# Output projection of a mixer that starts with the heads' blocks ahead of the gated products, with the turns of heads and groups between its pieces

## The chip, the cores and the metric

The kernel runs on one core of a Trainium2 chip. The metric is the device time of one execution in microseconds (us). TensorE (PE in the profile; PEld are its weight loads), VectorE (DVE), ScalarE (ACT) and GpSimd (POOL) each work through their own instructions in order and wait for one another on semaphores; SyncE (SP) issues the loads of the weight stream.

## What is computed

The kernel is two transformer blocks on a sequence of 1024 rows of width 1024, all in float32. The change lies in the mixer of the second block:

```python
proj = h @ w_mix_in[l]
q, k, v, u = jnp.split(proj, [ATTN_WIDTH, 2 * ATTN_WIDTH, 3 * ATTN_WIDTH], axis=-1)
attn = dilated_attention(q, k, v).astype(x.dtype)            # 8 heads of 64: 512 columns
...
# s5_mixer(u): 32 groups of 16 channels: 512 columns
y = jax.nn.gelu(y.reshape(B, S, SSM_WIDTH))
return y * jax.nn.sigmoid(y @ w_glu.astype(f32) + b_glu.astype(f32))
...
mixed = jnp.concatenate([attn, ssm], axis=-1) @ w_mix_out[l]
x = x + rms_norm_2(mixed, mix_post_g[l])
```

The output projection `mixed` sums over 1024 channels. The first 512 come from the attention heads, the last 512 from the gated groups.

## The kernel before

**Products.** Every large product is made in three matmuls (lines 126, 127, 128, in `products`): each operand is kept as a high part and the rest (`hi` and `lo`), and hi·hi, hi·lo and lo·hi are summed in PSUM. ACT makes the high part with a copy, DVE then makes the rest with a subtraction (for a weight unit that is `make_hi`, L117, and `make_lo`, L121). PSUM has eight banks of 128x512.

**Weight stream.** All large weights come in units of 128x1024 (512 KB), in one fixed order, through two staging buffers `raw`. SP issues the load of unit n when unit n-2 is ready, that is when its `make_lo` has ended (semaphore `unit_ready`). For this mixer the stream has two units for the gate (`glu_unit(0)`, `glu_unit(1)`, written to `glu_w`) and then eight for the output projection (called `mixo`, slots `A[:, 0]` to `A[:, 7]` of `region_a`). Two blocks of 128 channels share a unit, and the second four units are the other 512 output columns.

**Attention** (`att_pe`, `att_act`, `att_dve`). A loop over 64 pairs (head, row tile) has scores, the maximum, the exponential, transposes of the probabilities (L1642), and the sum of values (`values`, L1652), whose result DVE scales into `O` (`att_o`, L1719; semaphore `at_o`). Between them stand the steps of the state-space groups (L1422 to L1431), whose last result ACT writes to `U` (L1463, semaphore `s5_g`).

**Turns.** `O` and `U` have rows on the partitions; the products need channels there. So PE turns each of them in eight pieces: a piece q is four 128x128 transposes into one PSUM bank, for block j = q // 2 and half of the rows q % 2. For the heads (L1673), ACT copies the piece to `B` (`region_b`, L1707), DVE writes its rest (L1740). The PE turns piece q when piece q-2 has been read (`ot_lo`), as there are two banks. For the groups (L1499), ACT applies GELU (L1520, semaphore `yt_f`) and after every second piece makes the high part (L1524); DVE makes the rest (L1539, `yt_lo`) in `YH`, the second half of `region_a`.

**Gate and projection.** `glu_pe` waits for all of that and has 8 groups of 12 matmuls (32x3 in all). After each, ACT applies the sigmoid (L1530, `gl_s`), DVE multiplies (L1547), ACT and DVE split the result into blocks 4 to 7 of `B` (L1533, L1549, `gl_lo`). Then `wide_pe` makes the projection: for each of the 8 channel blocks i, six row tiles of the first output half, 18 matmuls a block and 144 in all, in PSUM banks 0 to 5; then the ten other (row tile, half) pairs with 24 matmuls each. ACT and DVE reach `wide_hi(act, mixo, range(8))` and `wide_lo(dve, mixo, range(8))` after all of the gate's work.

Of the kernel before, what the change touches and what calls it, by code (L numbers as in the profile page):

```python
# [5 lines left out]
P = 128  # L6
S = 1024
D = 1024
NT = S // P
KD = D // P  # L10
HALF = 512
# [33 lines left out]
def program(nc, x, p, stream, cols, rows, gate_mats, pool_mats, inv_count, ssm_g, ssm_bc, x_mid, ssm_mid, att_mid, out):  # L45
    f32 = mybir.dt.float32
# [6 lines left out]
    with ctx:  # L53
# [1433 lines left out]
        def eighths(X, half):  # L1487

            return X.rearrange("p (c t) -> p t c", t=GT)[:, 4 * half:4 * half + 4, :]

        def glu_pe(pe):
            pe.wait_ge(s5_g, 8)
            for q in range(8):
                j, half = divmod(q, 2)
                if q >= 2:
                    pe.wait_ge(yt_f, q - 1)
                for t in range(4):
                    tt_ = 4 * half + t
                    last = nc.tensor.transpose(ps[:, 2 + q % 2, t * P:(t + 1) * P],  # L1499
                                               U[:, tt_, j * P:(j + 1) * P], ident[:, :])  # L1500
                last.then_inc(yt_tr, 1)
            pe.wait_ge(ot_lo, 8)
            pe.wait_ge(yt_lo, 8)
            pe.wait_ge(unit_ready, U_GLU + 2)
            for g in range(8):
                j, half = divmod(g, 2)
                if g >= 4:
                    pe.wait_ge(gl_s, g - 3)
                slot = glu_w[:, j // 2]
                for k in range(4):  # L1510
                    c0 = (j % 2) * HALF + k * P
                    last = products(ps[:, (0, 1, 4, 5)[g % 4], :], lambda h: slot[:, h, c0:c0 + P],
                                    lambda h: YH[:, k, h, half * HALF:(half + 1) * HALF], k == 0, k == 3)
                last.then_inc(gl_done, 1)

        def glu_act(act):
            for q in range(8):
                j, half = divmod(q, 2)
                act.wait_ge(yt_tr, q + 1)
                nc.scalar.activation(eighths(yf[:, j, :], half), ps[:, 2 + q % 2, :].rearrange("p (t c) -> p t c", t=4),  # L1520
                                     ACT.Gelu_apprx_tanh).then_inc(yt_f, 1)
                if half:
                    act.wait_ge(yt_f, q + 1)
                    nc.scalar.activation(YH[:, j, 0, :], yf[:, j, :], ACT.Copy).then_inc(yt_hi, 1)  # L1524
            for g in range(8):
                j, half = divmod(g, 2)
                act.wait_ge(gl_done, g + 1)
                if g >= 2:
                    act.wait_ge(gl_p, g - 1)
                nc.scalar.activation(sg[:, g % 2, :], ps[:, (0, 1, 4, 5)[g % 4], :], ACT.Sigmoid,  # L1530
                                     bias=c_("b_glu", j)).then_inc(gl_s, 1)
# [4 lines left out]
        def glu_dve(dve):  # L1536
            for j in range(4):
                dve.wait_ge(yt_hi, j + 1)
                nc.vector.tensor_tensor(YH[:, j, 1, :], yf[:, j, :], YH[:, j, 0, :].bitcast(f32),  # L1539
                                        ALU.subtract).then_inc(yt_lo, 2)  # L1540
            for g in range(8):
                j, half = divmod(g, 2)
                cut = slice(half * HALF, (half + 1) * HALF)
                dve.wait_ge(gl_s, g + 1)
                if g >= 2:
                    dve.wait_ge(gl_lo, g - 1)
                nc.vector.tensor_tensor(pr_[:, g % 2, :], yf[:, j, cut], sg[:, g % 2, :], ALU.mult).then_inc(gl_p, 1)  # L1547
                dve.wait_ge(gl_hi, g + 1)
                nc.vector.tensor_tensor(B[:, 4 + j, 1, cut], pr_[:, g % 2, :], B[:, 4 + j, 0, cut].bitcast(f32),  # L1549
                                        ALU.subtract).then_inc(gl_lo, 1)  # L1550

# [83 lines left out]
        def att_pe(pe):  # L1635
# [31 lines left out]
            pe.wait_ge(at_o, NA)  # L1667
            for q in range(8):
                j, half = divmod(q, 2)
                if q >= 2:  # L1670
                    pe.wait_ge(ot_lo, q - 1)
                for t in range(4):
                    last = nc.tensor.transpose(ps[:, q % 2, t * P:(t + 1) * P],  # L1673
                                               O[:, 4 * half + t, j * P:(j + 1) * P], ident[:, :])
                last.then_inc(ot_tr, 1)

        def att_act(act):
            def rest(n):
# [10 lines left out]
            for n in range(NA):  # L1689
# [6 lines left out]
                if n:  # L1696
                    rest(n - 1)
                    ssm_step_act(act, n - 1)
            link_act(act, nc.scalar.activation(small[:, 1:2], eps, ACT.Gelu_apprx_tanh))
            rest(NA - 1)  # L1700
            ssm_step_act(act, NA - 1)
            for u in range(2):
                hi_of(act, glu_unit(u))
            for q in range(8):
                j, half = divmod(q, 2)
                act.wait_ge(ot_tr, q + 1)
                nc.scalar.activation(B[:, j, 0, half * HALF:(half + 1) * HALF], ps[:, q % 2, :],  # L1707
                                     ACT.Copy).then_inc(ot_hi, 1)

        def att_dve(dve):  # L1710
            link = lambda ins: link_dve(dve, ins)
# [11 lines left out]
            for n in range(NA):  # L1723
# [10 lines left out]
            for u in range(2):  # L1734
                lo_of(dve, glu_unit(u))
            for q in range(8):
                j, half = divmod(q, 2)
                dst = B[:, j, :, half * HALF:(half + 1) * HALF]
                dve.wait_ge(ot_hi, q + 1)
                nc.vector.tensor_tensor(dst[:, 1, :], ps[:, q % 2, :], dst[:, 0, :].bitcast(f32),  # L1740
                                        ALU.subtract).then_inc(ot_lo, 1)


        mix_out = sem("mix_out")
# [255 lines left out]
        def _(act):  # L2000
# [47 lines left out]
        def _(dve):  # L2048
# [20 lines left out]
            proj_dve(dve)  # L2069
            att_dve(dve)  # L2070
            glu_dve(dve)
            wide_lo(dve, mixo, range(8))
# [7 lines left out]
        def _(pe):  # L2080
# [12 lines left out]
            glu_pe(pe)  # L2093
            wide_pe(pe, mixo, lambda i: pe.wait_ge(gl_lo, max(2, 2 * i - 6)), n_ffn2)
            feed_pe(pe, ffn2, n_ffn2, ({}, {}))


# [102 lines left out]
```

## Time and profile before

| | |
|---|---|
| time, median of 3 runs | 3254.61 us (3253.44 to 3259.25) |
| time of the profiled execution | 3254.53 us |
| its span | 3252.7 us (1.8 us of the time lies outside it) |
| mean granted TensorE clock | 0.976 |
| PE busy | 3089.1 us, 95% |
| DVE, ACT busy | 1380.0 us (42%), 868.3 us (27%) |
| last pair of the attention to the first product of the projection | 2345.16 to 2400.07 us |

The span is the time from the first to the last recorded instruction; all times below are us from its start. A granted clock of 1.0 is TensorE at full speed, 0.5 half of it. A busy PE is not a PE at its peak, since the ends of overlapping matmuls are modelled; the distance between two starts says more than the duration.

### The profile page before, as it was taken

To read this page: it belongs to the slowest core of one execution; us is meant where nothing else is said; L and a number is where in the kernel's file an instruction comes from. 1 tells how busy PE (TensorE), PEld (TensorE's weight loads), DVE (VectorE), ACT (ScalarE), POOL (GpSimd) and SP (SyncE) were. 2 spreads that over 40 slices of the span, in tenths; PEclk is the share of its full clock that TensorE was granted. 3 is DMA by queue.
4 is the path that set the end of the run, shared out by engine and by line. 5 is a ranking of instruction groups with operands and counts; after the bars stand their busy time and mean duration, and the time that the engine had idled before them with its cause. 6 is when DMAs were issued, how large, how long until landed. Compare 5 with 4: busy or idle time off the path is not lost.

```text
span 3252.7 us, 36883 instructions
## 1 busy us (share of the span) xinstructions
PE 3089.1 (95%) x14144; PEld 2546.1 (78%) x14144; DVE 1380.0 (42%) x1783; ACT 868.3 (27%) x1316; POOL 408.2 (13%) x1012
## 2 busy tenths in 40 slices
PE   7999999999998989999999989988888999999997
PEld 5777888888887777888888878877767888888885
DVE  5654444444445443333333363244435233333335
ACT  5523222211123342111121241144434211121112
POOL 0000000000000004888800000011101000000001
PEclk9999999999999999999999999989989999999998
DMA  3121111111111121232211221111113111111113
GB/s 121 39 78 65 59 52 52 45 39 45 52 52 39 52 72 48 90 109 83 88 45 64 97 85 65 70 66 48 38 65 117 59 46 40 51 58 45 39 52 117
DMA packets 54410, 206.99 MB, mean 64 GB/s; under 512 B 7216, under 2 KB 7984, under 8 KB 52000
## 3 DMA queue, kind: packets, MB, share of 16 engines
q1 hardware_dynamic: 37440, 136.33, 12.1%
q0 software_dynamic: 16864, 69.22, 5.8%
q8 instruction: 70, 1.15, 0.1%
q14 instruction: 36, 0.29, 0.0%
HBM read 173.15 MB, written 31.20 MB: 63 GB/s over the span
## 4 chain that ended last, share of the span: by engine, by line
PE 90%; DVE 5%; ACT 2%; issue 2%; DMA 0%; SPq 0%; POOL 0%; DVEq 0%; ACTq 0%
PE ps L126 28%; PE ps L128 27%; PE ps L127 27%; PE ps L1652 2%; PE ps L262 1%; PE ps L1616 1%; PE ps L1642 1%; DVE acc L815 1%; DVE region_b L121 1%; PE ps L1422 1%; DVE acc L177 1%; DVE acc L185 1%; PE ps L1417 0%; ACT region_b L117 0%; PE ps L1429 0%
## 5 line engine op out<-in xcount | busy, mean ns | idle before, releaser
L126 PE MATMUL ps<-region_a,region_b 128*128 128x512 f32 x1664 | 659.3, 396 | 19.4 <-DVE region_a L221 9.8
L127 PE MATMUL ps<-region_a,region_b 128*128 128x512 f32 x1664 | 651.7, 392 | 0.0
L128 PE MATMUL ps<-region_a,region_b 128*128 128x512 f32 x1664 | 651.4, 391 | 0.0
L815 DVE TENSOR_TENSOR acc<-acc,ps 128x1024 f32<-128x1024 f32 x288 | 351.1, 1220 | 332.6 <-PE ps L128 332.6
L126 PE MATMUL ps<-region_b,region_a 128*128 128x512 f32 x1088 | 433.3, 398 | 17.3 <-DVE region_b L121 9.9
L127 PE MATMUL ps<-region_b,region_a 128*128 128x512 f32 x1088 | 428.7, 394 | 0.0
L128 PE MATMUL ps<-region_b,region_a 128*128 128x512 f32 x1088 | 428.7, 394 | 0.0
L121 DVE TENSOR_TENSOR region_b<-raw,region_b 128x1024 fp32r<-128x1024 f32 x176 | 216.1, 1243 | 394.8 <-ACT region_b L117 394.4
L126 PEld LDWEIGHTS ps<-region_a,region_b 128*128 128x128 f32 x1664 | 314.9, 189 | 87.6 <-issue 10.0
L128 PEld LDWEIGHTS ps<-region_a,region_b 128*128 128x128 f32 x1664 | 314.7, 189 | 65.9
L127 PEld LDWEIGHTS ps<-region_a,region_b 128*128 128x128 f32 x1664 | 315.0, 189 | 64.8 <-issue 1.7
L126 PE MATMUL ps<-region_b 128*128 128x512 f32 x896 | 353.3, 394 | 8.6 <-DVE acc L811 4.8
L127 PE MATMUL ps<-region_b 128*128 128x512 f32 x896 | 350.7, 391 | 0.0
L128 PE MATMUL ps<-region_b 128*128 128x512 f32 x896 | 350.7, 391 | 0.0
L126 PEld LDWEIGHTS ps<-region_b,region_a 128*128 128x128 f32 x1088 | 215.7, 198 | 61.0 <-issue 10.1
L128 PEld LDWEIGHTS ps<-region_b,region_a 128*128 128x128 f32 x1088 | 215.4, 198 | 40.9
L127 PEld LDWEIGHTS ps<-region_b,region_a 128*128 128x128 f32 x1088 | 215.9, 198 | 39.2
L117 ACT ACTIVATE region_b<-raw 128x1024 fp32r<-128x1024 f32 x176 | 181.5, 1050 | 160.0 <-DMA raw<-stream 130.1
L726 ACT ACTIVATE rtmp<-ps 128x512 f32<-128x512 f32 x88 | 52.7, 598 | 630.2 <-PE ps L128 630.1
L126 PEld LDWEIGHTS ps<-region_b 128*128 128x128 f32 x896 | 169.5, 189 | 45.3 <-DVE acc L811 5.2
L121 DVE TENSOR_TENSOR region_a<-raw,region_a 128x1024 fp32r<-128x1024 f32 x74 | 89.5, 1224 | 261.0 <-ACT region_a L117 261.0
L128 PEld LDWEIGHTS ps<-region_b 128*128 128x128 f32 x896 | 169.3, 189 | 35.4
(286 smaller groups left out, 3343.9 us busy)
## 6 DMA issues: line engine op xcount, KB each, us to landing
raw<-stream SPq DMA_DIRECT2D x252, 512.0 KB, 3.2
ssm_row<-ssm_mid POOLq DMA_DIRECT2D x8, 1632.0 KB, 7.1
x_mid<-acc POOLq DMA_DIRECT2D x24, 512.0 KB, 3.0
ssm_mid<-made_osc POOLq DMA_DIRECT2D x8, 1024.0 KB, 4.5
ssm_mid<-made_out POOLq DMA_DIRECT2D x8, 608.0 KB, 3.5
acc<-x SPq DMA_DIRECT2D x8, 512.0 KB, 7.9
rold<-x POOLq DMA_DIRECT2D x16, 256.0 KB, 3.6
old_a<-x_mid POOLq DMA_DIRECT2D x8, 512.0 KB, 8.6
```

The lines of the kernel that those rows point to most:

```text
L117: nc.scalar.activation(slot[:, 0, :], raw[:, odd, :], ACT.Copy).then_inc(hi_done, 1)
L121: nc.vector.tensor_tensor(slot[:, 1, :], raw[:, odd, :], slot[:, 0, :].bitcast(f32), ALU.subtract).then_inc(unit_ready, 1)
L126: nc.tensor.matmul(psum, lhs(0), rhs(0), start=first, stop=False)
L127: nc.tensor.matmul(psum, lhs(0), rhs(1), start=False, stop=False)
L128: return nc.tensor.matmul(psum, lhs(1), rhs(0), start=False, stop=last)
L177: nc.vector.scalar_tensor_tensor(out=acc[:, t, :], in0=acc[:, t, :], scalar=rinv_post[:, t:t + 1], in1=gb[:, N.post, :], op0=ALU.mult, op1 ...
L185: nc.vector.scalar_tensor_tensor(out=a, in0=a, scalar=N.factor, in1=N.old(t), op0=ALU.mult, op1=ALU.add).then_inc(N.sem["res"], 1)
L262: last = nc.tensor.transpose(ps[:, 6 + d % 2, t * P:(t + 1) * P], xn[:, t, d * P:(d + 1) * P], ident[:, :])
L726: nc.scalar.activation(rtmp[:, half, :], ps[:, up_bank(c, j, half), :], ACT.Silu).then_inc(F.sem["ge"], 1)
L815: nc.vector.tensor_tensor(acc[:, t, :], acc[:, t, :], src, ALU.add).then_inc(F.sem["de"], 1)
L1422: last = nc.tensor.matmul(bank[i], zt[:, s - 4, i * P:(i + 1) * P], zt[:, 2, i * P:(i + 1) * P], start=True, stop=True)
L1652: last = nc.tensor.matmul(ps[:, 6, 0:HEAD_DIM], probT[:, n % 2, k, :], V[:, k, h * HEAD_DIM:(h + 1) * HEAD_DIM], start=k == 0, stop=k == i)
```

## The change

PE no longer turns all heads, then all groups, then makes the gate's products, then all of the projection. The heads' first two pieces (block 0, of heads whose values were long done) are turned before the last `values`, into banks 4 and 5. Two more follow. Then the projection begins with blocks 0 to 3 (the heads'), cut into eight pieces of three row tiles (9 matmuls each), with two turns behind each of the first six pieces: the heads' last four and the groups' eight, all in banks 6 and 7. Then come the gate's products, now in banks 6 and 7 in place of 0, 1, 4 and 5 (so a group waits for the sigmoid of the group before the last), and then blocks 4 to 7 of the projection. What stands behind them is the same.

On ACT and DVE the high part and the rest of gate unit 0 move ahead of the attention's last step, those of `mixo` units 0 and 1 stand among the heads' turns (behind pieces 2 and 4), and those of units 2 and 3 among the gate's results (behind groups 1 and 3). Units 4 to 7 stay behind the gate. The stream's order is the same; a unit's load is still tied to the unit two ahead of it being ready. The number of matmuls, copies and loads does not change.

```diff
+        TURN_BANKS = (4, 5) + (7, 6) * 7
+
+        def turn_heads_pe(pe, q):
+
+            j, half = divmod(q, 2)
+            if q < 2:
+                pe.wait_ge(at_pt, NA)
+            elif q == 2:
+                pe.wait_ge(s5_g, NB)
+            elif q == 3:
+                pe.wait_ge(at_o, NA)
+            else:
+                pe.wait_ge(ot_lo, q - 1)
+            pe.wait_ge(at_o, 2 * NT * (j + 1))
+            for t in range(4):
+                last = nc.tensor.transpose(ps[:, TURN_BANKS[q], t * P:(t + 1) * P],
+                                           O[:, 4 * half + t, j * P:(j + 1) * P], ident[:, :])
+            last.then_inc(ot_tr, 1)
+
+        def turn_groups_pe(pe, q):
+
+            j, half = divmod(q, 2)
+            pe.wait_ge(*((yt_f, q - 1) if q >= 2 else (ot_lo, 7 + q)))
...
         def glu_pe(pe):
...
+            pe.wait_ge(yt_f, 8)
             pe.wait_ge(yt_lo, 8)
-            pe.wait_ge(unit_ready, U_GLU + 2)
             for g in range(8):
                 j, half = divmod(g, 2)
-                if g >= 4:
-                    pe.wait_ge(gl_s, g - 3)
+                if g >= 2:
+                    pe.wait_ge(gl_s, g - 1)
...
+        def mixo_pe(pe):
...
+            turns = [lambda q=q: turn_heads_pe(pe, q) for q in range(4, 8)]
+            turns += [lambda q=q: turn_groups_pe(pe, q) for q in range(8)]
+            turn_heads_pe(pe, 2)
+            turn_heads_pe(pe, 3)
+            for k in range(4):
+                pe.wait_ge(unit_ready, U_MIXO + k // 2 + 1)
+                pe.wait_ge(ot_lo, 2 * k + 2)
+                for part_of in range(2):
+                    for t in range(3 * part_of, 3 * part_of + 3):
+                        part(0, t, k, k == 0, False)
+                    for turn in turns[4 * k + 2 * part_of:4 * k + 2 * part_of + 2]:
+                        turn()
+            glu_pe(pe)
+            for k in range(4, KD):
+                pe.wait_ge(unit_ready, U_MIXO + k // 2 + 1)
+                pe.wait_ge(gl_lo, 2 * k - 6)
+                for t in range(6):
+                    ins = part(0, t, k, False, k == KD - 1)
...
         def glu_act(act):
+            for q in range(8):
+                turn_heads_act(act, q)
+                if q == 2 or q == 4:
+                    wide_hi(act, mixo, [q // 2 - 1])
...
                 nc.scalar.activation(B[:, 4 + j, 0, half * HALF:(half + 1) * HALF], pr_[:, g % 2, :],
                                      ACT.Copy).then_inc(gl_hi, 1)
+                if g == 1 or g == 3:
+                    wide_hi(act, mixo, [2 + g // 2])
...
+            turn_heads_pe(pe, 0)
+            turn_heads_pe(pe, 1)
             values(NA - 1)
...
+            lo_of(dve, glu_unit(0))
             finish(NA - 1)
-            for u in range(2):
-                lo_of(dve, glu_unit(u))
...
+            lo_of(dve, glu_unit(1))
...
-            wide_hi(act, mixo, range(8))
+            wide_hi(act, mixo, range(4, 8))
```

PE's instructions from the last `values` on, before. `att_o` are the heads' outputs, `u` the groups', `ident` the identity of a transpose; the waits of an instruction stand in brackets.

```order
L1652 MATMUL ps<-v,probT 128x64 [waits at_o,at_pt]
L1652 MATMUL ps<-v,probT 128x64 x7
L1673 MATMUL ps<-ident,att_o 128x128 [waits at_o]
L1673 MATMUL ps<-ident,att_o 128x128 x7
L1673 MATMUL ps<-ident,att_o 128x128 [waits ot_lo]
L1673 MATMUL ps<-ident,att_o 128x128 x3
```

The same place in the changed kernel:

```order
L1506 MATMUL ps<-ident,att_o 128x128 [waits at_o,at_pt]
L1506 MATMUL ps<-ident,att_o 128x128 x3
L1733 MATMUL ps<-v,probT 128x64 [waits at_o,at_pt]
L1733 MATMUL ps<-v,probT 128x64 x7
L1506 MATMUL ps<-ident,att_o 128x128 [waits at_o,s5_g]
L1506 MATMUL ps<-ident,att_o 128x128 x3
L1506 MATMUL ps<-ident,att_o 128x128 [waits at_o]
L1506 MATMUL ps<-ident,att_o 128x128 x3
L126 MATMUL ps<-region_a,region_b 128x512 [waits ot_lo,unit_ready]
L127 MATMUL ps<-region_a,region_b 128x512
L128 MATMUL ps<-region_a,region_b 128x512
```

A piece of the heads' turn now stands ahead of the last `values`, and the first matmul of the projection stands behind the fourth turn, with a wait for a weight unit.

ACT's instructions at the same place, before (`glu_w` the gate's weights, `L1699` the load of GELU's table, L1463 the last group's result):

```order
L1699 ACT_TABLE_LOAD
L1699 ACTIVATE small<-small 128x1
L1684 ACTIVATE probT<-ps 128x1024 [waits at_pv,at_tr,act_chain]
L1463 ACTIVATE u<-ps 128x4x8x16 [waits s5_y]
L117 ACTIVATE glu_w<-raw 128x1024 [waits at_s,raw_full0]
L117 ACTIVATE glu_w<-raw 128x1024 [waits at_s,raw_full1]
L1707 ACTIVATE region_b<-ps 128x512 [waits ot_tr] x8
```

And in the changed kernel:

```order
L117 ACTIVATE glu_w<-raw 128x1024 [waits at_s,raw_full0]
L1773 ACT_TABLE_LOAD
L1773 ACTIVATE small<-small 128x1
L1757 ACTIVATE probT<-ps 128x1024 [waits at_pv,at_tr,act_chain]
L1463 ACTIVATE u<-ps 128x4x8x16 [waits s5_y]
L117 ACTIVATE glu_w<-raw 128x1024 [waits at_s,raw_full1]
L1577 ACTIVATE region_b<-ps 128x512 [waits ot_tr] x3
L117 ACTIVATE region_a<-raw 128x1024 [waits at_pv,raw_full0]
L1577 ACTIVATE region_b<-ps 128x512 [waits ot_tr] x2
L117 ACTIVATE region_a<-raw 128x1024 [waits at_pv,raw_full1]
L1577 ACTIVATE region_b<-ps 128x512 [waits ot_tr] x3
```

Gate unit 0 moved ahead of the table load, and the first two units of the projection (`region_a<-raw`) moved in among the eight copies of the heads' pieces. DVE's queue is cut in the same way.

## Rows read from the trace of the kernel before

**Rows 1.** The page: span, and the chain that ended last, by engine.
```profile
span 3252.7 us, 36883 instructions
PE 90%; DVE 5%; ACT 2%; issue 2%; DMA 0%; SPq 0%; POOL 0%; DVEq 0%; ACTq 0%
```

**Rows 2.** Busy time by stretch: PE, PEld, DVE, ACT, POOL, granted clock, DMA share, GB/s.
```profile
2347.10:2357.00 9.90, 6.30 (x34) 5.08 (x34) 6.60 (x10) 4.07 (x7) 0.00 (x0) 0.75 0.32 106
...
2367.20:2371.50 4.30, 0.00 (x0) 0.03 (x1) 2.42 (x2) 4.13 (x4) 1.11 (x2) 0.50 0.64 229
2371.50:2395.60 24.10, 24.10 (x96) 19.46 (x96) 9.56 (x14) 9.26 (x14) 0.00 (x0) 0.91 0.01 4
```

**Rows 3.** PE in order of time: start, us, instruction, idle time before and its releaser.
```profile
2345.16 1.97 PE L1652 MATMUL ps<-v,probT 128*128 128x64 f32 x16 [0.54 <-DVE att_o L1719]
2347.58 1.09 PE L1673 MATMUL ps<-ident,att_o 128*128 128x128 f32 x8 [0.45 <-DVE att_o L1719]
...
2371.50 0.77 PE L126 MATMUL ps<-region_a,glu_w 128*128 128x512 f32 x1 [4.35 <-issue]
...
2376.18 0.39 PE L128 MATMUL ps<-region_a,glu_w 128*128 128x512 f32 x1
...
2395.22 0.39 PE L128 MATMUL ps<-region_a,glu_w 128*128 128x512 f32 x1
2400.07 0.77 PE L126 MATMUL ps<-region_a,region_b 128*128 128x512 f32 x1 [4.46 <-DVE region_a L121]
...
2403.48 0.39 PE L128 MATMUL ps<-region_a,region_b 128*128 128x512 f32 x1
```

**Rows 4.** ACT in order of time, the same columns.
```profile
2342.92 0.60 ACT L1463 ACTIVATE u<-ps 128x512 f32<-128x512 f32 x1 [3.16 <-PE ps L1431]
...
2348.27 1.09 ACT L1707 ACTIVATE region_b<-ps 128x512 fp32r<-128x512 f32 x2 [2.86 <-PE ps L1673]
...
2360.93 2.04 ACT L1520 ACTIVATE yf<-ps 128x512 f32<-128x512 f32 x2
2362.99 1.06 ACT L1524 ACTIVATE region_a<-yf 128x1024 fp32r<-128x1024 f32 x1
...
2370.09 1.28 ACT L1530 ACT_TABLE_LOAD   x1
2376.61 0.69 ACT L1530 ACTIVATE sg<-ps,col 128x512 f32<-128x512 f32 x1 [5.23 <-PE ps L128]
```

**Rows 5.** DVE in order of time, the same columns.
```profile
2344.73 0.28 DVE L1719 TENSOR_SCALAR att_o<-ps,stats 128x64 f32<-128x64 f32 x1 [4.44 <-PE ps L1652]
...
2347.44 2.35 DVE L121 TENSOR_TENSOR glu_w<-raw,glu_w 128x1024 fp32r<-128x1024 f32 x2
2349.70 1.28 DVE L1740 TENSOR_TENSOR region_b<-ps,region_b 128x512 fp32r<-128x512 f32 x2
...
2370.18 1.22 DVE L1539 TENSOR_TENSOR region_a<-yf,region_a 128x1024 fp32r<-128x1024 f32 x1 [1.78 <-ACT region_a L1524]
2377.33 0.69 DVE L1547 TENSOR_TENSOR pr<-yf,sg 128x512 f32<-128x512 f32 x1 [5.93 <-ACT sg L1530]
```

**Rows 6.** DVE and ACT on the projection's units, in order of time.
```profile
2398.70 2.36 DVE L121 TENSOR_TENSOR region_a<-raw,region_a 128x1024 fp32r<-128x1024 f32 x2 [0.25 <-ACT region_a L117]
2403.31 1.06 ACT L117 ACTIVATE region_a<-raw 128x1024 fp32r<-128x1024 f32 x1 [3.70 <-DMA raw<-stream]
```

**Rows 7.** PE where a norm's turns stand between products, in order of time.
```profile
2510.52 0.60 PE L262 MATMUL ps<-ident,xn 128*128 128x128 f32 x4
...
2511.66 0.60 PE L262 MATMUL ps<-ident,xn 128*128 128x128 f32 x4
```

**Rows 8.** Two stretches of 2 us within the turns, columns as in rows 2.
```profile
2356.00:2358.00 2.00, 2.00 (x11) 2.00 (x11) 1.02 (x2) 1.30 (x3) 0.00 (x0) 0.50 0.00 0
2360.00:2362.00 2.00, 0.64 (x4) 0.40 (x4) 0.88 (x1) 2.00 (x3) 0.00 (x0) 1.00 0.00 0
```

**Rows 9.** ACT on the last unit of the projection, in order of time.
```profile
2416.86 1.06 ACT L117 ACTIVATE region_a<-raw 128x1024 fp32r<-128x1024 f32 x1 [1.03 <-DMA raw<-stream]
```

More of the change, by code:

```diff
@@ L1489, in eighths @@
             return X.rearrange("p (c t) -> p t c", t=GT)[:, 4 * half:4 * half + 4, :]
[L1491 to L1502 removed]
+        TURN_BANKS = (4, 5) + (7, 6) * 7
[17 more added lines that the diff above has]
+            pe.wait_ge(*((yt_f, q - 1) if q >= 2 else (ot_lo, 7 + q)))
+            for t in range(4):
+                tt_ = 4 * half + t
+                last = nc.tensor.transpose(ps[:, TURN_BANKS[8 + q], t * P:(t + 1) * P],
+                                           U[:, tt_, j * P:(j + 1) * P], ident[:, :])
+            last.then_inc(yt_tr, 1)
+        def glu_pe(pe):
+            pe.wait_ge(yt_f, 8)
             pe.wait_ge(yt_lo, 8)
[L1504 removed]
             for g in range(8):
                 j, half = divmod(g, 2)
[L1507 to L1508 removed]
+                if g >= 2:
+                    pe.wait_ge(gl_s, g - 1)
                 slot = glu_w[:, j // 2]
@@ L1511, in glu_pe, with part @@
                     c0 = (j % 2) * HALF + k * P
-                    last = products(ps[:, (0, 1, 4, 5)[g % 4], :], lambda h: slot[:, h, c0:c0 + P],
+                    last = products(ps[:, 6 + g % 2, :], lambda h: slot[:, h, c0:c0 + P],
                                     lambda h: YH[:, k, h, half * HALF:(half + 1) * HALF], k == 0, k == 3)
                 last.then_inc(gl_done, 1)
+        def mixo_pe(pe):
+            def part(half, t, k, first, last):
+                slot = mixo.slots[4 * half + k // 2]
+                return products(ps[:, (NT * half + t) % 6, :],
+                                lambda h: B[:, k, h, t * P:(t + 1) * P],
+                                lambda h: slot[:, h, (k % 2) * HALF:(k % 2 + 1) * HALF], first, last)
+            turns = [lambda q=q: turn_heads_pe(pe, q) for q in range(4, 8)]
[16 more added lines that the diff above has]
+                    ins = part(0, t, k, False, k == KD - 1)
+                    if k == KD - 1:
+                        ins.then_inc(mixo.done, 1)
+            for g in range(6, 2 * NT):
+                half, t = divmod(g, NT)
+                if t == 0:
+                    pe.wait_ge(unit_ready, U_MIXO + 8)
+                pe.wait_ge(mix_out, g - 5)
+                for k in range(KD):
+                    last = part(half, t, k, k == 0, k == KD - 1)
+                    if g == NT + 6 and k % 2:
+                        norm_pe_step(pe, n_ffn2, 0, k // 2)
+                    if g == NT + 7 and k % 2 == 0:
+                        norm_pe_step(pe, n_ffn2, 0, 4 + k // 2)
+                last.then_inc(mixo.done, 1)
@@ L1534, in glu_act @@
                                      ACT.Copy).then_inc(gl_hi, 1)
+                if g == 1 or g == 3:
+                    wide_hi(act, mixo, [2 + g // 2])
         def glu_dve(dve):
+            for q in range(8):
+                j, half = divmod(q, 2)
+                dst = B[:, j, :, half * HALF:(half + 1) * HALF]
+                dve.wait_ge(ot_hi, q + 1)
+                nc.vector.tensor_tensor(dst[:, 1, :], ps[:, TURN_BANKS[q], :], dst[:, 0, :].bitcast(f32),
+                                        ALU.subtract).then_inc(ot_lo, 1)
+                if q == 2 or q == 4:
+                    wide_lo(dve, mixo, [q // 2 - 1])
             for j in range(4):
@@ L1701, in att_act @@
             ssm_step_act(act, NA - 1)
-            for u in range(2):
[L1703 to L1708, printed above, removed]
+            hi_of(act, glu_unit(1))
         def att_dve(dve):
@@ L2071, in _ @@
             glu_dve(dve)
-            wide_lo(dve, mixo, range(8))
+            wide_lo(dve, mixo, range(4, 8))
             dve_mixo(dve, ffn2_norm_hooks(dve))
```

32 lines of the change are left out of this document (12 added, 20 removed).

## Prediction

> **What bounds the kernel now.** I read the page first. The chain that ended last is PE for 90% of the span [rows 1], so time is won only where PE stands still, runs at half clock, or is given less to do. The change gives it the same matmuls. Next I read busy time by stretch around the place of the change [rows 2]: from 2347.10 to 2357.00 PE is busy 6.30 of 9.90 us, from 2367.20 to 2371.50 not at all, and the granted clock is 0.75 and 0.50 there (1.0 is 2.4 GHz, 0.50 is 1.2 GHz; 0.75 is a mean over both). Then PE in order of time [rows 3]: the heads' turns begin at 2347.58, the gate's products at 2371.50 after 4.35 us of nothing, the projection at 2400.07 after 4.46 us of nothing. In this stretch PE is paced by others: ACT has a chain of two GELUs and a high part for each block (2.04 us and 1.06 us, one directly behind the other [rows 4]), DVE ends it [rows 5], and the wait at 2400.07 is for the first unit of the projection, whose high part and rest ACT and DVE make only after the gate [rows 6].
>
> What the work itself takes: the gate's 12th matmul starts at 2376.18, its 96th at 2395.22 [rows 3], 84 steps of **0.2267 us**. The first 11 steps took 4.68 us instead of 2.49 us, so restarting at half clock cost 2.19 us. In the projection the ninth matmul starts 3.41 us after the first, where eight steps are 1.81 us: 1.60 us lost. A turn between products costs 0.455 us of PE: between two turns of a norm, 1.14 us apart [rows 7], stand three matmuls (0.68 us). From 2347.58 the old order needs, at these prices, 16 turns (7.3 us), 96 matmuls (21.8 us) and the 144 of the first six tiles (32.6 us), 61.7 us. It ends at 2403.48 + 136 x 0.2267 = **2434.3**, which is 86.7 us. So 25 us stand open to be won, and the question is how much the new order leaves.
>
> **The change, step by step.** I replay the three queues with those durations.
>
> *Start.* The values of pair 62 end just before 2344.73, when DVE scales them [rows 5]. PE now turns heads' pieces 0 and 1 (2344.45 to 2345.36, 0.9 us), then the last values (16 steps, 1.8 us, the 1.97 us row without its end [rows 3]) to 2347.16, piece 2 at once, and piece 3 after DVE's last scaling, at 2347.7 to 2348.2. The two early pieces delay the last values by 0.5 us only, since PE waited there anyway. ACT has written `U` at 2343.5 [rows 4], so piece 2 does not wait for it. The high part of gate unit 0 and the table load now lie in ACT ahead of the last `probT`, about 1 us later than before, but PE's state-space step and values of pair 62 cover it. On DVE the rest of gate unit 0 fills 2345.0 to 2346.2, where DVE had nothing to do.
>
> *The first unit.* That rest lets SP load `mixo` unit 0. The price of a load is in [rows 6]: two rests of units take 2.35 us from 2398.70, so the first is ready at 2399.93, and ACT starts on the unit that this let in at 2403.31: 3.38 us. Here: 2346.2 + 3.4 gives 2349.65; high part to 2350.7 (1.03 us); DVE, which meanwhile has the rest of gate unit 1 (2347.6 to 2348.8) and pieces 0 to 2 (0.64 us each, to 2350.8), makes the unit's rest to 2352.0. PE stands still from 2348.2 to 2352.05: **3.9 us**, a new wait for a weight unit. Behind it stands everything on PE. I expect half clock afterwards, as after 4.46 us at 2400.07, at the same 1.6 us.
>
> *Pieces with turns.* Piece one (9 matmuls, 2.04 + 1.6 us) ends at 2355.7, turns 4 and 5 at 2356.6, the next piece at 2358.65, turn 6 at 2359.1. Turn 7 needs bank 6, thus DVE's rest of head piece 5. In front of it ACT and DVE have `mixo` unit 1, behind piece 4: ACT 2356.33 to 2357.96, then piece 5 to 2358.56; DVE unit 1 to 2359.2, piece 5 to 2359.86. PE waits **0.9 us** and turns piece 7 until 2360.4. Unit 1 is needed only at block 2. Block 1 with groups' turns 0 to 3 lasts 4.08 + 1.82 us to 2366.3, block 2 with turns 4 to 7 as long, to 2372.2, block 3 without turns to **2376.3**.
>
> *GELU chain.* ACT can start GELU at 2363.1, after the first group turn. Four blocks at 1.98 + 1.02 us end at 2375.1, DVE's last rest (1.22 us) at 2376.4. Every turn it wants is there, since two pieces with four turns take PE 5.9 us and ACT 6.0 us for four GELUs with two high parts. The gate starts at 2376.47: PE and ACT arrive together, 0.15 us of wait. The table load of 1.28 us is hidden by the gate's first group of 2.72 us.
>
> *Gate.* 96 x 0.2267 = 21.8 us at full clock, to 2398.2, without the 2.19 us of a cold start. Two banks instead of four: group g waits for the sigmoid of group g-2, which ends 0.9 us after that group (sigmoid 0.69 us), while a group takes 2.72 us. Units 2 and 3 in ACT and DVE (1.03 and 1.2 us) delay the next sigmoids to at most 1.7 us after their products, and lag does not build up. No wait.
>
> *Rest.* Blocks 4 to 7 need 72 x 0.2267 = 16.3 us, to **2414.55**. Block 4 needs groups 0 and 1 of the gate, done long before; block 7 needs the last, ready at 2401.2 against 2410.5. Units 4 to 7 are made after the gate. Before, the last of the eight was made from 2416.86 on [rows 9], 19 us after the high part of the first. Now only four are left behind the gate, with two of them already loaded; begun at 2400.5 and at the same pace they are made by about 2412, and PE wants them behind 48 more matmuls, at 2425.4. All later work hangs on PE's `mixo.done` and DVE's copies and keeps its distances.
>
> **Sum.** 2434.3 - 2414.55 = 19.8 us. Against the profiled execution's 3254.53 us that is **3234.7 us**; this execution stands 0.08 us under the median of the runs, so nothing is to be corrected.
>
> **Bounds of what is not shown.** The clock after 3.9 us of standing still: if it does not fall, 1.6 us more gain (21.4, 3233.1); if the restart costs as much as the gate's, 2.19, 0.6 less. The first load: each us later costs 1 us; the transfer could overlap other loads, I take up to 2 us. Turn 7 and the joint arrival at the gate: 1.1 us together, which a slightly different order of arrival could double. That spans 3233 to 3239.
>
> **A rule against the change.** The transposes carry the clock here, as [rows 8] show: from 2356 to 2358 PE is busy 2.00 of 2.00 us with eleven transposes at clock 0.50, and at 2360 to 2362 the clock is 1.00, with nothing but transposes in between. The Trainium skill ("TensorE: Matmul & The Clock Gate", Part 4: PE-mode transpose) says the opposite, that full clock does not engage for transposes because they do not count as busy work. By that rule the pieces with turns might stay at half clock, and the result would be that of the second rival below; the trace disagrees with it.
>
> **Rivals.**
> *Smaller gain by a longer wait.* The new wait for unit 0, or GELU's chain, costs 3 to 13 us more than replayed: if ACT's order (unit 1 behind piece 4, whose turn stands behind the first products) held the turns back for a whole piece each time, 2 to 4 us for each of three places. For it: three engines hand over in turn at each piece. Against: each hand-over is in the rows. Time 3238 to 3248.
> *Half clock among the turns.* If the clock stayed at 0.50 over blocks 0 to 2, 54 matmuls cost 0.2 us more each and twelve turns 0.45 us more each, together 16.2 us instead of the 1.6 us counted, while the 0.9 us wait vanishes. Gain 6.2 us, 3248.3 us. Against it: in [rows 7] the mix of three matmuls and a turn runs at full speed, and here it is 9 to 2.
> *Slower.* The clock stays low for good: a matmul costs 0.2 us more, so from 99 matmuls at half clock on, the whole gain is gone; over blocks 0 to 3 and the gate (168) and the twelve turns it costs 39 us against 19.8 + 1.6: 3272 us. Against it: both restarts in [rows 3] are over in under 5 us, and the new order has fewer gaps.
> *It does nothing.* Something behind the projection had waited for another thing, and the gain goes into that wait. PE's share of the chain [rows 1] and the stream, which runs two units ahead of its use, speak against it; 3250 to 3256 us.
>
> **How the numbers follow.** Forecast 0.80 (3233 to 3238); smaller gain 0.12; half clock 0.03; nothing 0.03; slower 0.02. The predicted time is the forecast's 3234.7. What a measurement tells from no change is 0.2%, 6.5 us: faster means under 3248.1. The forecast and the smaller gain lie there, and part of the others: faster 0.95, within 0.2% 0.03, slower 0.02. The range reaches from the lower bound with a little scatter, 3232, to 3240 in the smaller-gain case.
>
> **What would show it.** In the changed kernel's trace: about 3.9 us of PE waiting for DVE on a `region_a` unit before the first product near 2352; a wait near 0.9 us before the heads' turn 7; the gate's first matmul near 2376.5, with under 1 us of idle ahead and full clock; no idle time between gate and block 4; the first six tiles done near 2414.6. It is wrong if PE waits at the group turns for GELU, if the clock is 0.5 beyond 2357, or if a wait of more than 1 us appears before the gate or before a unit after 2414.

## The result and the profile after

The changed kernel took 3235.41 us (median of 5 runs, 3232.16 to 3240.03), the kernel before 3253.44 us beside it (5 runs, 3249.81 to 3259.25): ratio 0.9944, 95% interval 0.993 to 0.9959, 18 us faster. Two later sets of 5 runs gave 0.9945 and 0.9941. The profiled execution took 3240.03 us, its span is 3238.2 us against 3252.7 [rows 1].

The page of the changed kernel:

```profile
span 3238.2 us, 36891 instructions
PE 3086.3 (95%) x14144; PEld 2543.7 (79%) x14144; DVE 1379.6 (43%) x1783; ACT 867.8 (27%) x1316; POOL 408.2 (13%) x1012
...
PE 90%; DVE 5%; ACT 2%; issue 2%; DMA 1%; SPq 0%; DVEq 0%; POOL 0%; ACTq 0%
```

PE bounds it as before. Executions differ by microseconds ahead of the changed place and behind it, so I compare one **stretch**: from the start of the values of pair 62 to DVE's first copy of the projection's banks. Before, it runs from 2342.72 to 2431.13, **88.41 us**; after, from 2346.45 to 2417.73, **71.28 us**: 17.1 us won. Its two ends before, then its end after (its start is the first row of the fence behind them):

```profile
2342.72 1.90 PE L1652 MATMUL ps<-v,probT 128*128 128x64 f32 x16
2431.13 4.09 DVE L1763 COPY acc<-ps 128x512 f32<-128x512 f32 x6 [11.95 <-PE ps L128]
```

```profile
2417.73 4.09 DVE L1825 COPY acc<-ps 128x512 f32<-128x512 f32 x6 [1.07 <-PE ps L128]
```

PE in order of time, the changed kernel (start, us, instruction, idle time and releaser; it answers to [rows 3]):

```profile
2346.45 1.90 PE L1733 MATMUL ps<-v,probT 128*128 128x64 f32 x16
2348.18 1.04 PE L1506 MATMUL ps<-ident,att_o 128*128 128x128 f32 x8
2349.06 1.90 PE L1733 MATMUL ps<-v,probT 128*128 128x64 f32 x16
2350.79 1.27 PE L1506 MATMUL ps<-ident,att_o 128*128 128x128 f32 x8
2356.70 0.79 PE L126 MATMUL ps<-region_a,region_b 128*128 128x512 f32 x1 [4.64 <-DVE region_a L121]
...
2360.71 1.41 PE L1506 MATMUL ps<-ident,att_o 128*128 128x128 f32 x8
2361.87 0.48 PE L126 MATMUL ps<-region_a,region_b 128*128 128x512 f32 x1
...
2365.17 0.66 PE L1506 MATMUL ps<-ident,att_o 128*128 128x128 f32 x4 [0.53 <-DVE region_b L1612]
...
2382.76 0.47 PE L126 MATMUL ps<-region_a,glu_w 128*128 128x512 f32 x1 [0.94 <-DVE region_a L1618]
2383.06 0.40 PE L127 MATMUL ps<-region_a,glu_w 128*128 128x512 f32 x1
```

One long wait is new, 4.64 us for unit 0. The first nine products take 4.01 us behind it (2356.70 to 2360.71), and turns 4 and 5 1.16 us. The gate starts behind 0.94 us and at full clock, its second product 0.30 us behind the first; before it stood 4.35 us ahead of the gate and ran 11 steps at half clock. Between gate and projection's last blocks nothing waits, where 4.46 us stood. The clock, in windows (columns as in [rows 2]):

```profile
2354.00:2356.00 2.00, 0.00 (x0) 0.00 (x0) 0.85 (x2) 1.54 (x2) 0.00 (x0) 0.66 0.60 211
2356.00:2358.00 2.00, 1.30 (x3) 1.11 (x4) 1.25 (x2) 0.00 (x0) 0.00 (x0) 0.50 0.18 35
...
2360.00:2362.00 2.00, 2.00 (x12) 1.70 (x11) 0.00 (x0) 0.29 (x1) 0.00 (x0) 0.64 0.00 0
2362.00:2364.00 2.00, 2.00 (x11) 1.60 (x10) 1.40 (x2) 1.74 (x3) 0.00 (x0) 1.00 0.00 0
```

It falls while PE stands. A mean of 0.64 from 2360 to 2362 means half clock until about 2361.4, and from there on it is full. ACT on unit 0 and on the GELUs (answers to [rows 4]):

```profile
2354.33 1.06 ACT L117 ACTIVATE region_a<-raw 128x1024 fp32r<-128x1024 f32 x1 [2.30 <-DMA raw<-stream]
...
2368.38 2.20 ACT L1588 ACTIVATE yf<-ps 128x512 f32<-128x512 f32 x2 [1.92 <-PE ps L1516]
2370.61 1.06 ACT L1593 ACTIVATE region_a<-yf 128x1024 fp32r<-128x1024 f32 x1
2371.58 2.22 ACT L1588 ACTIVATE yf<-ps 128x512 f32<-128x512 f32 x2
```

Two GELUs now take 2.20 us; they took 2.04 us in [rows 4].

### The profile page after: what moved, and what is told of

Its sections match the earlier page's. It is cut to its first block, busy times and chain, and to the rows that moved or that the text cites. A ratio compares the mean times of both kernels' runs of the same rounds, so it can differ in the third digit from the quotient of the medians.

```text
span 3238.2 us, 36891 instructions
## 1 busy us (share of the span) xinstructions
PE 3086.3 (95%) x14144; PEld 2543.7 (79%) x14144; DVE 1379.6 (43%) x1783; ACT 867.8 (27%) x1316; POOL 408.2 (13%) x1012
## 3 DMA queue, kind: packets, MB, share of 16 engines
q0 software_dynamic: 16864, 69.22, 5.9%
## 4 chain that ended last, share of the span: by engine, by line
PE 90%; DVE 5%; ACT 2%; issue 2%; DMA 1%; SPq 0%; DVEq 0%; POOL 0%; ACTq 0%
PE ps L126 27%; PE ps L127 27%; PE ps L128 27%; PE ps L1733 2%; PE ps L262 1%; PE ps L1697 1%; PE ps L1723 1%; DVE acc L815 1%; DVE region_b L121 1%; PE ps L1422 1%; DVE acc L177 1%; DVE acc L185 0%; PE ps L1429 0%; ACT region_b L117 0%; PE ps L1417 0%
```

## Experiments

The letters A and B are set anew in each expectation. Diffs are against the changed kernel unless said otherwise. Where a time is called a stretch, it is the one above, read from the profiled execution.

**e1, the units alone.** The kernel before, with only the first two `mixo` units moved into the gate (an order between the sigmoids' reads and the projection's writes of their banks had to be added):

```diff
@@ wide_pe
+                    if i == 0 and t in (0, 4) and W.n0 == U_MIXO:
+                        pe.wait_ge(gl_s, 6 + t // 2)
@@ glu_act (glu_dve the same with wide_lo)
+                if g == 1 or g == 3:
+                    wide_hi(act, mixo, [g // 2])
-            wide_hi(act, mixo, range(8))
+            wide_hi(act, mixo, range(2, 8))
```

> The kernel before, with one part of the change alone: the high part and the rest of the projection's units 0 and 1 are made among the gate's results (behind groups 1 and 3) and no longer behind the gate; nothing on PE is moved, apart from two waits for the gate's sigmoids that the banks need. I measure the stretch from the start of the values of pair 62 to the first copy of a projection tile out of PSUM: 88.4 us in the trace of before, 71.3 us in the one of the changed kernel, 17.1 us apart. Theory A (as in the prediction: idle time and restarts of PE are what was won): the 4.46 us of waiting at 2400.07 and the 1.60 us of restart go, the stretch is 82.3 us (81.5 to 83.5) and the kernel 6 us faster than before, so a third of the gain needs no new order on PE. Rival B (the units were not what the projection really waited for; gl_lo, the last gated product, ends only 3 us later than the gate and would stop it instead): under 3 us gained.

Measured: ratio 0.9982 (0.9973 to 0.9991), 3249.45 against 3255.85 us; stretch 2338.34 to 2420.46, 82.12 us. PE's waits in it (us in total, times, longest):

```profile
PE ps L126 <- issue: 4.3, 1, 4.3
PE ps L1501 <- ACT yf L1522: 3.4, 4, 1.4
PE ps L1679 <- DVE region_b L1746: 2.4, 3, 1.3
```

The wait between gate and projection is gone, the one ahead of the gate stays. Of the 88.41 us, 6.3 are won by the earlier units alone: 4.46 of standing still and the slow restart behind it (1.60). The other 10.8 us of the 17.1 come from the rest of the change.

**e2, the turns not mixed in.** Everything of the change, but all turns stand ahead of block 0:

```diff
+            for turn in turns:
+                turn()
             for k in range(4):
...
-                    for turn in turns[4 * k + 2 * part_of:4 * k + 2 * part_of + 2]:
-                        turn()
```

> The changed kernel without turns between pieces: the heads' last four and the groups' eight turns stand ahead of block 0 of the projection, then blocks 0 to 3, then the gate. Theory A (the pieces are worth it because PE works while ACT does copies and GELU): the turns alone run at ACT's and DVE's pace, about 12 us for the groups and 6 to 8 us for the heads, and only their tail lies under blocks 0 to 3; stretch 78.5 us (77 to 81), so 7 us of the 17 are lost and the kernel is about 11 us faster than before. PE idle ahead of the gate is zero. GELU pieces take 1.01 us each again (2.03 for two) while PE stands, if it is PE's work that slows them to 1.10. Rival B (blocks 0 to 3 ahead of the gate win it all, whatever stands between them): stretch 71 to 73 us.

Measured: ratio 0.9963 (0.9949 to 0.9976), 3245.72 us; stretch 2348.55 to 2426.24, 77.69 us. PE's waits:

```profile
PE ps L1506 <- DVE region_b L1612: 4.2, 3, 2.3
PE ps L1516 <- ACT yf L1588: 2.3, 3, 1.0
PE ps L1516 <- DVE region_b L1612: 0.6, 1, 0.6
```

These 7.1 us stand between turns, for ACT and DVE to empty the two banks. Mixing is worth 77.69 - 71.28 = 6.4 us here, and up to 8.5 against the change's other executions (below). Little of it is standing still: the change has waits of 4.64, 0.53 and 0.94 us of its own, 6.1 in all, as its turns no longer fill the wait for unit 0. The larger part is the clock. In e2 the granted clock is 0.50 in every window of 2 us from 2358 to 2376, over nearly all of the twelve turns and the first products; in the change's first execution it is at half for some 7 us, most of them a wait and nine products. Two turns in e2, at half clock:

```profile
2371.17 2.05 PE L1516 MATMUL ps<-ident,u 128*128 128x128 f32 x8 [0.97 <-ACT yf L1588]
```

Eight transposes take 2.05 us there and 1.04 in the change, behind products. The side forecast on GELU came out too: where PE mostly waits, two GELUs take 2.03 us again.

**e3, the wait filled with transposes.** 36 transposes of the identity into the still free bank 0, behind turn 3 (extra work, no result used):

```diff
+            for i in range(36):
+                nc.tensor.transpose(ps[:, 0, i % 4 * P:(i % 4 + 1) * P], ident[:, :], ident[:, :])
```

> The changed kernel with 36 more transposes of the identity into PSUM bank 0 (nobody reads them) in the 4.64 us in which PE waits for unit 0; about 4.1 us of work at full clock. Theory A (the half clock behind the wait comes from the idle time, and transposes hold the clock): the first nine products take 2.1 us where they took 4.0, the two turns behind them 0.8 us where they took 1.16; the granted clock stays 1.0; stretch 69.2 us (68.8 to 70). Rival B (transposes do not count as work for the clock, or the clock falls for another reason): granted clock 0.5 for the first nine products as before, stretch 71.3 us or a little more.

Measured: ratio 0.9934 (0.9921 to 0.9948), 3235.22 us; stretch 2345.96 to 2415.15, 69.19 us. PE, and two windows:

```profile
2351.41 4.09 PE L1546 MATMUL ps<-ident 128*128 128x128 f32 x36
2356.32 0.50 PE L126 MATMUL ps<-region_a,region_b 128*128 128x512 f32 x1 [0.81 <-DVE region_a L121]
...
2358.50 1.04 PE L1506 MATMUL ps<-ident,att_o 128*128 128x128 f32 x8
```

```profile
2352.00:2354.00 2.00, 2.00 (x21) 2.00 (x19) 1.79 (x3) 0.06 (x1) 0.00 (x0) 1.00 0.55 164
...
2356.00:2358.00 2.00, 1.68 (x7) 1.42 (x8) 0.86 (x2) 0.00 (x0) 0.00 (x0) 1.00 0.31 59
```

Nothing but transposes runs from 2352 to 2354, and the clock stays 1.00; the nine products take 2.18 us instead of 4.01, the turns behind them 0.79 instead of 1.16: 2.2 us of restart saved, as the stretch shows (2.1). The Trainium skill ("TensorE: Matmul & The Clock Gate", Part 4: PE-mode transpose), by which transposes do not count as busy work, is contradicted by these rows.

**e4, banks of the projection's later tiles for turns 4 and 5**, so that they need no product ahead of them:

```diff
-        TURN_BANKS = (4, 5) + (7, 6) * 7
+        TURN_BANKS = (4, 5, 7, 6, 3, 4) + (7, 6) * 5
...
             turn_heads_pe(pe, 3)
+            turn_heads_pe(pe, 4)
+            turn_heads_pe(pe, 5)
...
+                    if k == 0 and part_of:
+                        pe.wait_ge(ot_lo, 6)
```

> The changed kernel with the heads' turns 4 and 5 made at once behind turn 3, in banks 3 and 4, which are free until the second piece of block 0; the later turns move up by one piece. Theory A (the waits that the order leaves are bank waits and GELU's late start): two turns (1.2 us) leave the busy stretch, the 0.53 us wait before turn 7 and the 0.94 us before the gate go; PE idle before unit 0 shrinks by 0.8 us as DVE and PE finish nothing sooner there; stretch 69.0 us (68.5 to 70). Rival B (the two copies now stand in ACT's and DVE's queues ahead of unit 1 or 0 and delay it): the first product starts later or block 2 waits, stretch 71 us or more.

Measured: ratio 0.9942 (0.9929 to 0.9956), 3236.7 us; stretch 2345.94 to 2412.71, 66.77 us, 2.2 us better than expected, of which 1.0 is unit 0's load. The waits for unit 0 shrink to 1.92 us, those at turn 7 and at the gate are gone, and one of 0.64 us at turn 5's bank is new. The added copies did not delay unit 0, so rival B falls.

**e5, without the early turns**: `turn_heads_pe` of pieces 0 and 1 behind `values(NA - 1)` instead of ahead of it.

> The changed kernel with the heads' turns 0 and 1 behind the last values again, as before. Stretch as measured above (from the values of pair 62 to the first copy of a projection tile; 71.3 us in the changed kernel's trace, of which a load of unit 0 that took 4.3 us instead of 3.3 us made 1.0). Theory A (PE's start on the projection is set by the rest of gate unit 0 on DVE, the load and the two halves of unit 0, and not by PE): the two turns fall into PE's wait for unit 0, which shrinks by 0.9 us; stretch 71.3 us, or 70.3 us if the load takes 3.3 us. Rival B (turning early is part of what was won, as the prediction counted PE's path through it): 72 to 73 us.

Measured: ratio 0.9937 (0.9924 to 0.9951), 3237.39 us; stretch 2346.76 to 2417.55, 70.79 us. PE:

```profile
2349.20 1.97 PE L1733 MATMUL ps<-v,probT 128*128 128x64 f32 x16 [0.54 <-DVE att_o L1787]
2351.01 1.92 PE L1506 MATMUL ps<-ident,att_o 128*128 128x128 f32 x16
2356.44 0.79 PE L126 MATMUL ps<-region_a,region_b 128*128 128x512 f32 x1 [3.51 <-DVE region_a L121]
```

The wait is 1.13 us shorter than in the change's first execution: 0.57 is the quicker load (3.7 against 4.3 us), 0.56 is that PE gets to the wait later. A holds. The first product starts 2.37 us behind ACT's start on unit 0 here (2354.07 to 2356.44), and just so in the change (2354.33 to 2356.70) and in its two later executions; from there on the stretch takes 61.1 us here and 61.0 there. Turning two pieces early only moves time out of a wait that is there anyway, and no trace shows a gain from it.

**e6, GELU's output walked differently**: its writes go to four adjacent elements at a time, where the change writes every eighth element. What ends up in `yf` is the same; PSUM is now read with a step of 128 elements:

```diff
-                nc.scalar.activation(eighths(yf[:, j, :], half),
-                                     ps[:, TURN_BANKS[8 + q], :].rearrange("p (t c) -> p t c", t=4),
+                nc.scalar.activation(yf[:, j, :].rearrange("p (c t) -> p c t", t=GT)[:, :, 4 * half:4 * half + 4],
+                                     ps[:, TURN_BANKS[8 + q], :].rearrange("p (t c) -> p c t", t=4),
```

> The changed kernel with GELU's result walked in another order: it writes runs of four neighbouring elements and reads PSUM with a step of 128 elements, where it read PSUM in order and wrote single elements 8 apart. The result is the same. In the changed kernel two GELUs take 2.20 us (2.03 us where PE stands still), while two plain copies of the same size take 1.09 us. Theory A (the scattered write costs the second half of it, and PE's reads of the same memory the 0.17 us on top): two GELUs take 1.4 us or less, the 0.94 us wait before the gate goes, stretch 70.3 us (69.3 with a quick load). Rival B (GELU itself or the step in PSUM costs it): 2.2 us or more, stretch 71.3 us or, if the step in PSUM is slow, above.

Measured: ratio 0.9938 (0.9923 to 0.9953), 3236.22 us; stretch 2342.0 to 2412.01, 70.01 us. ACT:

```profile
2363.92 1.09 ACT L1588 ACTIVATE yf<-ps 128x512 f32<-128x512 f32 x2 [1.92 <-PE ps L1516]
2365.04 1.06 ACT L1593 ACTIVATE region_a<-yf 128x1024 fp32r<-128x1024 f32 x1
2366.86 1.09 ACT L1588 ACTIVATE yf<-ps 128x512 f32<-128x512 f32 x2 [0.76 <-PE ps L1516]
```

Two GELUs take 1.09 us instead of 2.20, as long as two plain copies; the step in PSUM costs nothing that shows. ACT now waits 0.76 us for PE at each later pair, and PE's wait at the gate is gone: this is all that GELU's chain cost, some 0.9 us, though it became 1.1 us a block shorter.

**e7, e4's banks and 16 idle transposes together.**

> Both mended: heads' turns 4 and 5 in free banks ahead of the projection (alone: stretch 66.8 us with a load of 3.3 us) and 16 transposes of the identity behind them in the 1.9 us that are left of PE's wait (alone, with 36 of them: 69.2 us with a load of 4.1 us, clock 1.00 throughout). Theory A (the clock falls for the idle time, transposes hold it): the first nine products take 2.1 us instead of 3.2 us, the turns behind them 0.8 instead of 1.1 us; stretch 65.4 us (66.4 us if the load takes 4.3 us); the kernel 22 to 24 us faster than before. Rival B (the restart falls somewhere else, for the clock answers to more than the last wait): no more than 0.5 us from 66.8 us.

Measured: ratio 0.9934 (0.992 to 0.9948), 3236.34 us; stretch 2346.87 to 2413.18, 66.31 us; wait for unit 0 1.13 us, clock 1.00 in every window from 2352 to 2366. Against e4 only 0.5 us, with a load 0.9 us longer. The stretch is A's (66.4 us with a load of 4.3 us), and the nine products take 2.20 us. The kernel is not: 20.4 us under the kernel before beside it (3256.76 us), where A had 22 to 24. e9 to e12 look into that.

**e8, unit 0 let in later**: `lo_of(dve, glu_unit(0))` behind `finish(NA - 1)`.

> The changed kernel with one line turned round on DVE: the rest of gate unit 0 behind the scaling of the last values instead of ahead of it. Theory A (the rest of gate unit 0 lets the load of unit 0 start, and PE's start on the projection hangs on that load): unit 0 is 2.7 us later, and so is the first product: idle time 7.3 us (6.3 with a quick load), stretch 74.0 us (73.0). Rival B (something else, such as DVE's four rests in front of the unit's, holds the start): less than 1 us.

Measured: ratio 0.9943 (0.9929 to 0.9958), 3239.55 us; stretch 2344.28 to 2417.11, 72.83 us. PE:

```profile
2348.63 1.27 PE L1506 MATMUL ps<-ident,att_o 128*128 128x128 f32 x8
2356.08 0.79 PE L126 MATMUL ps<-region_a,region_b 128*128 128x512 f32 x1 [6.18 <-DVE region_a L121]
```

A holds: the path runs through DVE's rest of gate unit 0, the load, and the high part and rest of `mixo` unit 0. With a load of 3.2 us the wait is 6.18 us, expected 6.3, and the first product again starts 2.37 us behind ACT's start on unit 0.

**e9 to e12, scatter, and the combined form.** On one chip: the changed kernel twice (e9, e11) and e7's kernel twice (e10, e12).

> The changed kernel itself, once more, so that it stands on one chip beside the form that combines the freed banks and the filled wait, since its median so far (3235.41 us) was taken beside other runs. Theory A (what the shorter stretch gains reaches the end of the kernel, and the medians so far are only blurred by some 3 us between executions): about 18 to 21 us under the kernel before, and 3.5 to 5 us above the combined form. Theory B (what is gained in this stretch beyond the change is given back later, in a wait or at the clock): the same time as the combined form within 1 us.

> Freed banks for turns 4 and 5 and sixteen idle transposes in the wait, together. Its stretch from the values of pair 62 to the projection's first copies took 66.31 us against 71.28 us for the change, of which up to 1.2 us can be the first unit's load. Theory A: 3.5 to 5 us under the median of the changed kernel on the same chip. Theory B: within 1 us of it. The stretch itself should again take 65.4 to 67.0 us.

> The changed kernel a third time, for the width of the scatter. Both theories: median within 1.5 us of its other set of this chip, the stretch 70.3 to 71.5 us, depending on whether the first unit's load takes 3.4 or 4.4 us; if a load of 3.4 us appears in the same kernel, the load's length belongs to the execution and not to the order of the program.

> The combined form a third time. Both theories: median within 1.5 us of its other set of this chip, the stretch 65.4 to 67.0 us. A: the four medians fall into two pairs 3.5 to 5 us apart. B: they do not.

| kernel | median us | ratio | stretch us | load of unit 0, issue to ACT's start | rest of the span behind the stretch |
|---|---|---|---|---|---|
| change, first | 3235.41 | 0.9944 | 71.28 | 4.3 | 820.5 |
| change, e9 | 3237.11 | 0.9945 | 69.19 | 3.1 | 823.7 |
| change, e11 | 3235.72 | 0.9941 | 69.22 | 3.1 | 820.7 |
| both, e7 | 3236.34 | 0.9934 | 66.31 | 4.3 | 823.0 |
| both, e10 | 3237.23 | 0.9939 | 66.38 | 4.1 | 821.4 |
| both, e12 | 3235.72 | 0.9938 | 65.48 | 3.2 | 824.7 |

The load's length belongs to the execution: the same program shows 4.3 and 3.1 us. With it the change's stretch came out at 69.2 us twice, under the 70.3 to 71.5 expected. The combined form wins 2.8 to 3.7 us in its stretch, and the four medians do not fall into A's two pairs. That is no proof of B. On this chip the mean of the change's ten executions lies 1.7 us above that of the combined form's eleven, with a 95% interval of about -1.4 to 4.8 us, in which both no gain and the whole of the stretch's gain lie.

What the traces show is where a gain can be lost again. Both forms have the same wait of 2.94 us ahead of a norm's turns, 48 us behind the stretch's end. PE in e9, then in e11:

```profile
2462.82 1.11 PE L262 MATMUL ps<-ident,xn 128*128 128x128 f32 x4 [2.94 <-DVE xn L208]
2463.58 0.78 PE L126 MATMUL ps<-region_a,region_b 128*128 128x512 f32 x1
```

```profile
2464.38 0.66 PE L262 MATMUL ps<-ident,xn 128*128 128x128 f32 x4 [2.94 <-DVE xn L208]
2464.79 0.47 PE L126 MATMUL ps<-region_a,region_b 128*128 128x512 f32 x1
```

Same kernel, same wait; in e9 PE goes on at half clock, in e11 at full. Counted over 20 us windows, e9 is 16 PE instructions behind e11 from there on, 16 x 0.2267 = 3.6 us; the rest of the span differs by 3.0 us. Every one of the 14 traces has this wait, and they part by it. Where PE goes on at half clock or falls to it within two products (before, e3, e6, e7, e9, e12), the rest behind the stretch is 821.6 to 824.7 us; where it goes on at full clock, 820.3 to 821.4 us. Of the combined form's three executions two fell there, of all others four of eleven. All three of the combined form also wait 0.6 to 0.7 us for an `acc` copy (L811) 170 us behind the stretch, where the change and e4 wait for nothing; this is some 0.7 us that the combined form gives back each time (821.4 us in e10 against 820.5 and 820.7). The execution e10 lost no more than that, and took 3232.6 us. Whether the combined form makes the clock fall more often, three executions can't tell, nor is it shown whether it beats the change.

## Why the prediction was right

The time was 3234.7 predicted, 3235.41 measured. That the two lie 0.7 us apart is partly luck: the five executions reach from 3232 to 3240 us, and beside the kernel before the gain is 18.0 us (18.3 and 19.7 in the two later sets), where 19.8 were predicted. The stretch is the better test. In its terms the prediction was 88.41 - 19.8 = 68.6 us; the three executions of the change show 71.28, 69.19 and 69.22. From start to start (us from the stretch's start; predicted times less 2342.72):

| PE reaches | predicted | first | e9 | e11 |
|---|---|---|---|---|
| first product | 9.33 | 10.25 | 9.10 | 9.04 |
| second piece, behind turns 4 and 5 | 13.88 | 15.42 | 13.67 | 13.62 |
| third piece, behind turns 6 and 7 | 17.68 | 19.14 | 17.07 | 17.13 |
| block 3 | 29.48 | 31.00 | 28.94 | 28.93 |
| gate | 33.75 | 36.31 | 34.22 | 34.21 |
| end of the stretch | 68.6 | 71.28 | 69.19 | 69.22 |

- **25 us open, filled by the new order**: right. e1 shows the units' part (6.3 us), e2 the mixing's (6.4 to 8.5), and what is left of e2's own 10.7 us, 4.4, is about the 4.3 us ahead of the gate, which the first blocks would cover. That last attribution is mine; no run separates it.
- **Wait for unit 0, 3.9 us**: 4.64, 3.48 and 3.42. The mechanism is e8's, and the 2.4 us from ACT's start on the unit to the first product came out as replayed (2.37). The term's size hangs on the load of 3.38 us [rows 6], which was 4.46 from the rest's end in the first execution (2349.87 to 2354.33) and 3.3 in the other two.
- **Restart 1.6 us**: the nine products and turns 4 and 5 took 5.17 us in the first execution, 4.57 and 4.58 in the others, against 2.97 in e3 at full clock: 2.2 and twice 1.6. In e9 and e11 the clock fell only in the middle of the nine products (the fourth still 0.8 us behind the first), and cost as much as in [rows 3], where it was low at the first.
- **Turn 7, 0.9 us**: 0.53, 0.19 and 0.35. Too large: turns 4 and 5 took 1.16, 1.56 and 1.46 us where I counted 0.91, so PE came to turn 7 later.
- **Gate, 0.15 us**: 0.94, 0.92 and 0.93, and 1.1 us from start to start, since the idle time counts only from the modelled end of the last product. This was a mis-sized term: I took 1.98 + 1.02 us a block after [rows 4]; beside a busy PE it takes 3.20 (2368.38 to 2371.58), and four blocks add the 0.8 us. In e6, with shorter GELUs, the wait is gone.
- **Products between turns**: right as a sum. A piece of nine took 2.16 us where I counted 2.04, as its first product starts 0.31 us ahead of the next, but the two turns behind it took 0.79 where I counted 0.91: 2.95 us a round, as replayed.
- **Gate 21.8 us with two banks, and no wait before blocks 4 to 7**: right, no wait of PE stands in the trace between 2382.76 and the end of the stretch.

So one term was mis-sized in all three executions, the gate's by 1.0 us from block 3 on. In e9 and e11 it is partly made up for by turn 7 (0.4 and 0.3 us) and the first product (0.2 and 0.3 us), which came earlier than replayed. In the first execution the long load adds 0.9 us and the restart 0.6.

That the first profiled execution took 3240 and the median nonetheless 3235.4 lies outside the stretch: it began 3.73 us later than before's. The twelve executions with the new order (e2 among them) began it between 2342.0 and 2348.6, the change itself at 2346.45, 2342.45 and 2343.98; what makes that scatter was not looked into. The span's gain of 14.5 us is 17.1 in the stretch, 1.1 behind it, less those 3.7.

The rivals: the smaller gain by a longer wait showed in one execution, by 0.7 us, not 3. Half clock among the turns didn't happen in the change; the clock rose within them. e2 shows what it looks like: with waits between the turns and no products, the clock stayed at 0.50 until products ran without a pause. In none of the runs did it stay low for good. One sign of being wrong was just met, the clock at 0.5 beyond 2357, that is 14.3 us into the stretch: in the first execution it was low until 15.0 us. That is 4.7 us behind a first product which itself came 0.9 us late, and not the half clock among the turns that the sign was meant for.

## What to carry to other kernels

Work that needs only half of its inputs can stand in front of the rest, and pay twice: it covers hand-overs between engines at the turns, and it removes the pauses after which PE runs at half clock. In e2 against the change the clock is the larger part of this, so idle time alone does not show the gain. Count for such a start the load that its first weights need, since nothing else stands ahead of them. A gain of 3 us in one place is not yet a gain of the kernel: compare the stretch in several executions, ask whether the scatter of the medians could show it at all, and look at the next waits, where clock and arrival times can take it back.

## What was not expected of the hardware

- Two GELUs in a row from PSUM to SBUF, 128x512 each: 2.03 us with PE mostly waiting (e2), 2.20 with PE busy (the change), both writing every eighth element, and 1.09 with four adjacent elements at a time (e6). The walk of the output doubles their time.
- The same program's 512 KB load took 3.1 or 4.3 us from issue to use, and 3.1 to 4.4 us over the eleven executions of the change and of e3 to e12. In the change's three executions a unit behind it was in flight too; what makes the difference stays open.
- After the same 2.94 us of standing still the clock was 0.50 in one execution of the change and 1.00 in another, and it fell there in six of the 14 traces. Whether a pause costs half clock can't be read from its length alone.
- Transposes without a pause hold the clock at 1.00 (e3). In e2, with PE making only turns and waiting up to 1.0 us between them, it stays at 0.50 for 14 us.
